# A hybrid decoder trunk on one core: three plain pairs in place of four at the start of each ConvGLU up-projection

## What is computed

```python
def conv_glu_ffn(h, w_up, conv_w, w_down):
    u = causal_depthwise_conv(h @ w_up, conv_w)     # 3 taps
    gate, val = jnp.split(u, 2, axis=-1)
    return (jax.nn.silu(gate) * val) @ w_down
...
f = conv_glu_ffn(rms_norm(x, ffn_pre_norm[layer]), ffn_w_up[layer], ffn_conv_w[layer], ffn_w_down[layer])
x = x + rms_norm(f, ffn_post_norm[layer])
```

## Time and profile before

| | us |
|---|---|
| median of 3 executions | 2599.65 (2599.0 to 2602.39) |
| the profiled execution | 2600.5 |
| its span in the profile | 2599.0 |
| PE busy in it | 2541.6 |
| feed-forward of the first layer (about) | 801 to 1430 |
| feed-forward of the second layer (about) | 1956 to the end |

### The profile page before, as it was taken

The page is one execution under the profiler, slowest core; times in us unless marked ns, Lnnn a source line. Parts: engine busy times, 40 slices in busy tenths (PEclk is TensorE's granted clock), DMA queues, the critical chain, the costliest instruction groups (busy, mean ns, idle before and its releaser), DMA issues. The chain is left out here.

```text
span 2599.0 us, 34381 instructions
## 1 busy us (share of the span) xinstructions
PE 2541.6 (98%) x12557; PEld 2107.5 (81%) x12557; DVE 1684.7 (65%) x1797; ACT 1189.4 (46%) x1738; POOL 1056.4 (41%) x689
## 2 busy tenths in 40 slices
PE   7899999999999999999999999999999999999998
PEld 5788888888787888888888788788887888888887
DVE  5667666776266766767548657557467676667446
ACT  6445445454443444444446434434443444444444
POOL 2443434443611787774003111111503777772004
PEclk9999999999899999999999999999999999999999
DMA  3235444333543232233766211110533223234666
GB/s 129 69 110 145 129 125 123 89 115 97 151 154 109 76 120 91 102 114 106 245 225 215 91 34 49 33 49 33 162 107 117 86 101 114 90 106 169 211 211 219
DMA packets 123390, 313.05 MB, mean 120 GB/s; under 512 B 13472, under 2 KB 27360, under 8 KB 119936
## 3 DMA queue, kind: packets, MB, share of 16 engines
q1 hardware_dynamic: 119936, 288.31, 32.7%
q0 software_dynamic: 3328, 23.07, 4.7%
HBM read 247.33 MB, written 110.13 MB: 138 GB/s over the span
## 5 line engine op out<-in xcount | busy, mean ns | idle before, releaser
L946 DVE TENSOR_TENSOR f_wlo<-f_raw,f_whi 128x1024 fp32r<-128x1024 f32 x154 | 205.0, 1340 | 134.0 <-ACT f_whi L644 133.3
L517 POOL TENSOR_TENSOR f_wlo<-f_raw,f_whi 128x512 fp32r<-128x512 f32 (+1 forms) x120 | 188.3, 1569 | 238.7 <-ACT f_whi L613 238.7
L644 ACT ACTIVATE f_whi<-f_raw 128x1024 fp32r<-128x1024 f32 x154 | 162.6, 1060 | 204.0 <-PE f_value L83 102.6
L517 POOL TENSOR_TENSOR f_wlo<-f_sums,f_whi 128x512 fp32r<-128x512 f32 x144 | 194.4, 1373 | 37.5 <-ACT f_whi L613 37.5
L573 POOL TENSOR_TENSOR f_xn<-f_acc,f_post 128x1024 f32<-128x1024 f32 x8 | 24.8, 3104 | 365.3 <-DVE f_acc L982 333.8
L687 ACT ACTIVATE f_kept<-f_part 128x512 f32<-128x512 f32 x108 | 64.5, 598 | 164.8 <-PE f_part L83 160.7
L613 ACT ACTIVATE f_whi<-f_sums 128x512 fp32r<-128x512 f32 x144 | 86.0, 623 | 87.9 <-POOL f_sums L523 87.9
L81 PE MATMUL f_part<-x_hi,f_whi 128*128 128x512 f32 x288 | 113.0, 392 | 0.0
L83 PE MATMUL f_part<-x_hi,f_wlo 128*128 128x512 f32 x288 | 113.0, 392 | 0.0
L81 PE MATMUL banks<-x_hi,g_whi_first 128*128 128x512 f32 x256 | 110.5, 432 | 2.5 <-POOL g_wlo_first L2068 2.5
L82 PE MATMUL f_part<-x_lo,f_whi 128*128 128x512 f32 x288 | 112.4, 390 | 0.0
(11 more groups left out here) (595 smaller groups left out, 8176.5 us busy)
## 6 DMA issues: line engine op xcount, KB each, us to landing
f_raw<-in_ffn_w_up SPq DMA_DIRECT2D x88, 512.0 KB, 3.8
f_raw<-operands_of SPq DMA_DIRECT2D x154, 256.0 KB, 2.9
f_raw<-w_sums SPq DMA_DIRECT2D x88, 256.0 KB, 3.0
w_sums<-in_ffn_w_down POOLq DMA_DIRECT2D x28, 768.0 KB, 8.5
f_raw<-in_ffn_w_down SPq DMA_DIRECT2D x66, 256.0 KB, 4.5
operands_of<-f_hid SPq DMA_DIRECT2D x22, 512.0 KB, 2.8
w_sums<-in_ffn_w_down SPq DMA_DIRECT2D x14, 768.0 KB, 7.7
w_sums<-w_sums SPq DMA_DIRECT2D x14, 768.0 KB, 6.1
```

The lines of the kernel that those rows point to most:

```text
L517: pool.tensor_tensor(part_of(w_lo, k), source, part_of(w_hi, k).bitcast(F32), ALU.subtract) \
L644: act.activation(step_part(w_hi, more_hi, d)[:, :], (raw + [last_raw])[r][:, :], ACT.Copy).then_inc(s_hi, 1)
L946: dve.tensor_tensor(step_part(w_lo, more_lo, d)[:, cols], source[:, cols], plain32(step_part(w_hi, more_hi, d)[:, cols]), ALU.subtract).th ...
```

## The change

`PLAIN` becomes 3, so pair 3 has seven products as well. Around that, the lists of the first pairs are rewritten:

- DVE makes the low parts of the plain tiles 2 to 5 (`plain_low`), POOL none of them. POOL makes the four weight sums of pair 3 first of all, before any low part, and waits for nothing but the two tiles.
- ACT's and DVE's lists for the first pairs are written out. The second half of the first token difference stands ahead of the convolution of pair 1's gate. The row sums of the first hidden tiles (three instead of four; the fourth comes later like those of other tiles) stand behind the token sums, in `spare` and `kept`. SP stores them in iteration 2 of its loop as before.
- DVE joins the gate of the first seven-product pair (`gate_joined`) before it convolves the last plain pair's value and multiplies it with the gate.
- The first copies of partial products wait for 7 or 8 token-sum parts, by the buffer that they write (`keep`).

The diff, without the removed rows of the long lists, which the kernel above shows:

```diff
-PLAIN = 4
+PLAIN = 3
 TEMP_OF = (0, 1, 2, 0, 1, 2, 0, 2)
...
     s_rows = sem("row_sum_made")
-    s_rstore = [sem(f"row_sum_stored{i}") for i in range(4)]
+    s_rstore = [sem(f"row_sum_stored{i}") for i in range(3)]
...
     SEVENTH, FOURTH = 5 * HALVED, 6 * HALVED
-    row_sums = [(R_F, 0), (R_D, 0), (R_S, 0), (R_G, 0), (R_F, 1), (R_D, 1), (R_S, 1)]
-    for i in range(2, HALVED):
+    row_sums = [(R_F, 0), (R_D, 0), (R_S, 0)]
+    for i in range(1, HALVED):
         row_sums += [(R_F, i), (R_G, i - 1), (R_D, i), (R_S, i)]
     row_sums.append((R_G, HALVED - 1))
-    FIRST_ROWS = 4
 
     def row_made(kind, i):
         return row_sums.index((kind, i)) + 1
 
     def row_home(kind, i):
 
-        if i == 0:
-            return {R_F: 0, R_D: 1, R_S: 2, R_G: 3}[kind], sums[:, {R_F: 0, R_D: 1, R_S: 2, R_G: 3}[kind], :]
         if kind == R_F or (kind, i) == (R_G, HALVED - 1):
             return 0, spare[:, near]
...
                 store_hidden(p - 1)
             if p == 2:
-                for kind in (R_F, R_D, R_S, R_G):
+                for kind in (R_F, R_D, R_S):
                     store_row(kind, 0)
-            if p == PLAIN:
-                store_row(R_F, 1)
             if p >= PLAIN:
                 for kind, i in ((R_F, p // 2), (R_G, p // 2 - 1)) if p % 2 else ((R_D, p // 2 - 1), (R_S, p // 2 - 1)):
...
                 pool.wait_ge(s_raw[n % FFN_RAWS], 16 * (n // FFN_RAWS) + 16)
+            if pair == PLAIN + 1:
+                pool.wait_ge(s_lo, task(PLAIN, A22) + 1)
             combine(0, gates[:, near], gates[:, far], ALU.add, 0)
             combine(1, sums[:, 0, :], values[:, near], ALU.subtract, made + 1)
-            lows((pair, A11))
             if pair == PLAIN:
-                lows((pair, S1), (pair, S2))
                 combine(2, values[:, near], gates[:, near], ALU.subtract, 0)
                 combine(3, values[:, far], sums[:, 1, :], ALU.subtract, made + 2)
-                lows((pair, A12), (pair, S3), (pair, A22))
+                pool.wait_ge(s_lo, 2 * PLAIN)
+                lows((pair, A11), (pair, S1), (pair, S2), (pair, A12), (pair, S3), (pair, A22))
                 return
+            lows((pair, A11))
             lows((pair - 1, S4), (pair, S2), (pair, S1))
             combine(2, values[:, near], gates[:, near], ALU.subtract, 0)
             lows((pair, S3), (pair, A22))
             combine(3, values[:, far], sums[:, 1, :], ALU.subtract, made + 2)
             lows((pair, A12))
 
-        for n in range(2, 2 * PLAIN):
-            low(n, raw[n % FFN_RAWS][:, :])
-        for s in s_rstore:
-            pool.wait_ge(s, 16)
         for pair in range(PLAIN, FT):
             operands(pair)
...
             else:
-                act.wait_ge(s_tlo, 8)
+                act.wait_ge(s_tlo, 8 if n == 2 else 7)
             act.activation(out, chain_ps, ACT.Copy).then_inc(s_kept, 1)
...
-        for p in range(PLAIN, FT):
+        high(2)
+        scaled_gate(0)
+        high(3)
+        token_sum_high(0, t1_hi[:, 0:2, :])
+        silu(0)
+        scaled_value(0)
+        token_sum_high(1, t2_hi[:, 0:2, :])
+        high(4)
+        token_sum_high(2, t4_hi[:, 0:2, :])
+        scaled_gate(1)
+        token_sum_high(3, t1_hi[:, 2:4, :])
+        high(5)
+        silu(1)
+        scaled_value(1)
+        high_operands(PLAIN, A11, S1, S2)
+        token_sum_high(4, t2_hi[:, 2:4, :])
+        high_operands(PLAIN, A12)
+        token_sum_high(5, t4_hi[:, 2:4, :])
+        scaled_gate(2)
+        token_sum_high(6, x_hi[:, 0:2, far])
+        high_operands(PLAIN, S3, A22)
+        keep(PLAIN, 0)
+        high_operands(PLAIN + 1, A11)
+        high_operands(PLAIN, S4)
+        token_sum_high(7, x_hi[:, 2:4, far])
+        keep(PLAIN, 1)
+        keep(PLAIN, 2)
+        silu(2)
+        scaled_value(2)
+        high_operands(PLAIN + 1, S2, S1, S3, A22, A12)
+        scaled_gate(PLAIN)
+        for p in range(PLAIN + 1, FT):
             more = p < FT - 1
             keep(p, 0)
-            if p > PLAIN:
-                silu(p - 1)
+            silu(p - 1)
             if more:
                 high_operands(p + 1, A11)
             high_operands(p, S4)
...
+        def plain_low(n):
+            dve.wait_ge(s_hi, n + 1)
+            dve.tensor_tensor(part_of(w_lo, n), raw[n % FFN_RAWS][:, :], plain32(part_of(w_hi, n)), ALU.subtract) \
+                .then_inc(s_lo, 1)
...
 
-        def joins(p):
-            def value_near():
-                dve.wait_ge(s_prod, task(p, A12) + 1)
-                dve.tensor_tensor(value_ps[p % 2][:, near], value_ps[p % 2][:, near], p1, ALU.add).then_inc(s_c11, 1)
-
+        def value_near(p):
+            dve.wait_ge(s_prod, task(p, A12) + 1)
+            dve.tensor_tensor(value_ps[p % 2][:, near], value_ps[p % 2][:, near], p1, ALU.add).then_inc(s_c11, 1)
+
+        def gate_joined(p):
             dve.wait_ge(s_kept, 3 * (p - PLAIN) + 3)
             dve.tensor_tensor(gate_ps[:, far], value_ps[p % 2][:, far], u3, ALU.add).then_inc(s_c22, 1)
             dve.wait_ge(s_prod, task(p, A22) + 1)
             dve.tensor_tensor(gate_ps[:, near], gate_ps[:, near], u3, ALU.add).then_inc(s_c21, 1)
-            conv(2 * p, gate_ps, gate, value_near)
 
         def rows_of(q):
-            if q == PLAIN:
-                row_sum(R_F, q // 2 - 1)
             if q % 2:
                 row_sum(R_F, q // 2)
...
-                conv(2 * p - 1, value_ps[(p - 1) % 2], hid[(p - 1) % 2])
+        plain_low(2)
+        conv(0, gate_ps, gate)
+        first_low(0)
+        second(0)
+        plain_low(3)
+        conv(1, value_ps[0], hid[0])
+        activated(0)
+        second_low(0)
+        fourth(0)
+        first_difference(1)
+        plain_low(4)
+        conv(2, gate_ps, gate)
+        fourth_low(0)
+        first_low(1)
+        plain_low(5)
+        conv(3, value_ps[1], hid[1])
+        activated(1)
+        second(1)
+        fourth(1)
+        second_low(1)
+        third_difference(0)
+        fourth_low(1)
+        third_low(0)
+        third_difference(1)
+        third_low(1)
+        conv(4, gate_ps, gate)
+        for kind in (R_F, R_D, R_S):
+            row_sum(kind, 0)
+        gate_joined(PLAIN)
+        conv(5, value_ps[0], hid[0])
+        activated(2)
+        rows_of(PLAIN)
+        conv(2 * PLAIN, gate_ps, gate, lambda: value_near(PLAIN))
+        for p in range(PLAIN + 1, FT):
+            value_far(p - 1)
+            conv(2 * p - 1, value_ps[(p - 1) % 2], hid[(p - 1) % 2])
             activated(p - 1)
             rows_of(p)
             if p == FT - 1:
                 hidden_low(0)
                 hidden_low(1)
-            joins(p)
+            gate_joined(p)
+            conv(2 * p, gate_ps, gate, lambda: value_near(p))
         hidden_low(2)
         value_far(FT - 1)
         hidden_low(3)
```

61 lines of the change are left out of this document (1 added, 60 removed).

## The result

| | before | after |
|---|---|---|
| median | 2600.7 us (6 runs beside it; the 3 shown ahead: 2599.65) | 2610.56 us |
| ratio, 95% interval | 1 | 1.0042 (1.0030 to 1.0053) |
| span of the profiled execution | 2599.0 | 2608.7 |
| PE busy, matmuls | 2541.6, 12557 | 2537.8, 12533 |

One of the six executions of the changed kernel took 5106.6 us and one of the four in experiment 7 took 5389.1; the ratios leave both out, and without them the two medians (2610.56 here, 2612.7 there) are 2610.5 and 2611.7.

A forecast was written before the change was run, and what follows sets the result against it. TensorE was taken to bound the kernel. Matmuls and waits removed, against two new waits and slow matmuls, gave +5.1 us in layer 1 and +5.9 in layer 2; +11.0 on the median 2599.65 made 2610.7 us, range 2603.5 to 2615.

The forecast's parts named there:

- The matmuls: Fourth pair of each feed-forward layer: 84 matmuls instead of 96, 2.74 us won a layer, 5.5 us in all.
- The old waits: TensorE's waits on gate convolutions in the feed-forward layers vanish: 0.3 us in the first, 1.2 us in the second.
- Wait A: TensorE's third gate tile waits for VectorE's convolution, slowed by turns with GpSimd's four sums: 0.9 us layer 1, 2.6 layer 2.
- Wait B: Product S2 of pair 4 waits for ScalarE's copy of A11, counted from the end of pair 3's S3: 5.6 us each layer.
- The lower bound: Pair 4's copy of A11 without turns: ScalarE's roundings chain ends at 12.6, a wait of 4.3 us.
- The clock: Behind Wait B the granted clock falls and eight matmuls run slow: 1.6 us a layer, bounds 0 and 1.6.
- Rival (1): Both layers as forecast but without the clock's fall: +7.8 us, 2607.5 us; chance 0.2.
- The second layer's sum: Second feed-forward layer, all terms: -3.94 + 2.6 + 5.6 + 1.6 = +5.9 us.
- The first layer's: First feed-forward layer, all terms: -3.04 + 0.9 + 5.6 + 1.6 = +5.1 us.
- (2): More waits of 1 us each, before S3 and A22 of pair 4, with upper bounds: 2613 to 2615.5 us; chance 0.1.
- (3): Light contention, engines seldom meet: Wait A nothing, Wait B 4.3 us; 2601.3 to 2604.5 us; chance 0.1.
- (4): Faster because Wait B isn't on the path; only matmuls and old waits count: -7.0 us, 2592.7 us; chance 0.1.

The follow-up runs named there:

- experiment 7: The changed kernel run once more, unaltered; 2612.7 us, ratio 1.0053 to the kernel before.
- kernel 4: The changed kernel with the low parts of plain tiles 2 to 5 made by GpSimd again, VectorE's four instructions removed; 2606.3 us in one run.
- experiments 2: The changed kernel with VectorE's two row sums of the last plain pair behind pair 3's gate convolution; 2608.2 us in one run.
- experiment 9: The changed kernel with both value joins of pair 3 and the first two copies of pair 4 earlier, row sums later; 2603.5 us, ratio 1.0017.
- experiment 3: The changed kernel with GpSimd's four weight sums of pair 3 held until pair 1's gate is convolved; 2610.1 us in one run.
- experiment 8: The lists of experiment 5 with the low parts of the plain tiles on GpSimd again; 2602.4 us, ratio 1.0012 to the kernel before.
- experiments 1: The changed kernel with pair 4's first copy ahead of later roundings and pair 3's scaled gate, value join ahead of the convolution; 2613.6 us, ratio 1.0059.
- experiment 6: Kernel 4 measured again, unaltered, with a new profile; 2611.1 us, ratio 1.0043 to the kernel before.
- experiment 5: The changed kernel with ScalarE's and VectorE's lists for pairs 0 to 5 rewritten, copies first, nothing left out; 2592.7 us, ratio 0.9975 to the kernel before.

## Why the prediction was right

**The matmuls.** 24 fewer, as said; TensorE's busy time fell by 3.8 us where 24 x 0.229 = 5.5 was charged, since slow matmuls count as busy as well.

**The old waits.** Gone. The prediction put the 0.9 us at the second pair of the second layer down to GpSimd's splits alone. The two profiles of kernel 4, which has these splits, show what else it needs: VectorE began after waiting 3.41 us for a transfer (f_taps) in the first, and there is no such wait of TensorE; it began after 4.76 us in the second, and TensorE waited 0.99. In before it was 4.72 us. In experiments 2 and 9, without the splits, VectorE waited 4.63 and 4.93 us and TensorE not at all there: it takes both, so the change does remove this wait, but it isn't there in every execution of a kernel with the splits.

**Wait A.** Forecast 0.9 and 2.6, measured 0.7 and 1.0. In the first layer every link is there: GpSimd's four sums, three of them at 2.16 to 2.29 us, fell into the stretch, and experiment 3 removed the wait by moving them. From the start of hidden x gate to the end of the convolution I had 16.9 us; it took 16.5, since a turn costs VectorE 0.96 (3.8 / 4) and not 1.1. That 0.9 and 0.7 lie so close is partly luck: hidden x gate began 17.4 us after the layer's first matmul (815.54 less 798.16) and not 17.0 as in before (817.94 less 800.98), with two splits more ahead of it, which the forecast left out. The two errors of 0.4 cancelled.

The price of a turn was partly luck as well. I had read VectorE's 3.25 us in the earlier trace rows as two turns. GpSimd's split ahead of the sum is not in those rows:

```profile
850.01 2.79 POOL L517 TENSOR_TENSOR f_wlo<-f_raw,f_whi 128x1024 fp32r<-128x1024 f32 x1 [11.11 <-ACT f_whi L613]
```

It ended at 852.80, and VectorE's operation 1.08 us later, at 853.88. That is one turn against one long split, as in experiment 8 (3.26 us). Halving it gave the price of a turn against a sum only because a sum is about half as long as such a split.

In the second layer the term was 1.6 us too large. The path of 16.5 us in place of 16.9 makes 0.4 of it; the rest is when VectorE begins. Its first token difference waits for the transfer of f_taps; before and after:

```profile
1959.91 1.23 DVE L857 TENSOR_TENSOR f_kept<-x_hi 128x1024 f32<-128x1024 f32 x1 [4.72 <-DMA f_taps<-in_ffn_conv_w]
```

```profile
1963.59 1.23 DVE L855 TENSOR_TENSOR f_kept<-x_hi 128x1024 f32<-128x1024 f32 x1 [3.32 <-DMA f_taps<-in_ffn_conv_w]
```

In the execution profiled after, VectorE waited 1.4 us less for it and had that head start. The list up to the third gate is the same in experiments 1, 7, 2 and 9: VectorE waited 3.19, 3.77, 4.63 and 4.93 us for the transfer, and TensorE 1.0, 1.3, 2.2 and 2.2 us at the third gate. I had taken VectorE's start from one execution of before; the third gate's wait has a spread of 1.2 us, and 2.6 is above all of it.

The Trainium skill (SBUF — State Buffer, "SBUF: two separate sides") calls it an exclusive lock, and the turns agree: 2.33 and 2.14 us where 1.22 is the bare duration. Its figure of about 115 ns for the handover ("A bandwidth-pool intuition that's wrong"), which the page measured on the descriptors of a DMA, doesn't show between these two engines' operations: GpSimd's first sum ended at 817.93 and VectorE's 1.22 us operation at 819.02, 1.09 us later. By that figure A would have been 2.0 and 3.7; the measured 0.7 and 1.0 speak against it. The same page has the lock only for VectorE operations with two SBUF inputs or in a two-port mode, and the rows agree: the value convolution, which reads one of its two tensors from PSUM, took 1.27 at 871.74 while GpSimd split without a pause:

```profile
871.53 2.55 POOL L512 TENSOR_TENSOR f_wlo<-f_sums,f_whi 128x512 fp32r<-128x512 f32 x2 [6.03 <-ACT f_whi L606]
```

**Wait B.** Forecast 5.6 each, measured 5.7 each. By its links from zero at 868.19, forecast against measured: hidden x gate starts at 5.6 (6.3), its duration 2.03 (1.95), gate convolution at 11.1 (11.5), join 1.20 behind it (1.20), copy 0.78 behind that (0.77), TensorE at 13.8 (14.1), needed at 8.2 (8.4, which is 882.30 less 5.70). The 0.65 us at the start are a link that I left out: the second join of the gate waits for product A22 and ran at 871.13, so VectorE couldn't convolve at 2.9. Hidden x gate and the row sums, at 1.58 and 1.57, gave 0.2 back. TensorE could go on 0.3 later than forecast and needed the copy 0.2 later, so the wait is closer to the forecast than either. The lower bound, ScalarE's chain at 12.6 (less 8.2 this is 4.4, not 4.3), was met by experiment 2 with 4.1.

**The clock.** Forecast 1.6 us a layer. Behind B the slow steps (0.38 to 0.43 us) add up to 1.3 us more than as many normal ones in the first layer and 1.6 in the second. The first step after the wait, 0.59 us in both, is not among them; behind a wait without the clock's fall it is 0.34 (experiment 9), so it adds about 0.3. Rival (1) falls.

**The second layer's sum:** -3.9 + 1.0 + 5.7 + 1.6 + 0.3 = +4.7, against +4.6 measured. **The first layer's:** -3.0 + 0.7 + 5.7 + 1.3 + 0.3 = +5.0 against +7.9. The rest, some 3 us, is mostly the pace: 1836 matmuls at 231.3 ns in place of 229.8 are 2.8 us. No term of the forecast held it, and experiment 6 shows that a kernel with the change can have either pace. What sets it stays open.

**The rivals.** (2) did not come: no wait at S3 or A22; the third token difference was in time. (Its sum in the prediction is off: all upper bounds together are 2613.8, and a wait of 1 us at each of two places in each layer makes 2617.8, not 2615.5.) The margin is thin: in experiments 3, 4 and 6 there are 0.2 to 1.0 us at a product that reads the far tokens, and in experiment 8, with VectorE later, there are 1.4 us at that product and 1.2 at the fourth gate's bank. (3) falls with the turns at full size. (4) fell because the copy held TensorE. Its number, 2592.7, is what experiment 5 measured, where the copies were put so that it doesn't. That the two agree to 0.1 us is chance, since waits of 0.3 and 0.7 us are left in experiment 5; but the median gain, 7.0 us, is about what the matmuls and the old waits hold.

## What to carry to other kernels

Work taken from the bottleneck engine also takes time away from all that hides beside it; the start of a pipeline, where the side engines catch up, is where it shows. Before a step is cut, add up what each side engine has to do ahead of the instruction that releases the bottleneck; a wait that only moves when one release is put earlier is a debt, to be spread over several steps. It isn't a fixed sum: shortening the longest chain gave 1.6 us back until the next chain was the longer. And where two engines take turns, moving work between them moves the place where they meet: look for that place too.
